# Reversing the column order of the moving operand and the PSUM output in all three-part products

## The reference, cut to what matters

```python
def first_block(x, ...):                 # HGRN2 mixer + conv mixer, then a conv SwiGLU FFN
    z = einsum('btd,dc->btc', rmsnorm(x), w_in)          # 1024 x 3584
    ...                                                   # chunkwise HGRN2, causal convolutions
    x = x + rmsnorm(concat(mix_a, mix_b) @ w_out)         # 1024 x 1024
    u = causal_dwconv(rmsnorm(x) @ ffn_w_up)              # 1024 x 5632
    return x + rmsnorm((silu(gate) * val) @ ffn_w_down)   # 2816 x 1024

def second_block(x, ...):                # two layers, each with a FFN before and after its mixer
    for l in range(2):
        h = h + 0.5 * swiglu(rmsnorm(h), wg, wu, wd)      # 1024 x 2816 twice, 2816 x 1024
        h = h + (pool_mixer(u) if l == 0 else mla_attention(u, ...))
        h = h + 0.5 * swiglu(rmsnorm(h), wg, wu, wd)
    return rmsnorm(h)
```

## Time and profile before

| | |
|---|---|
| median of 3 runs | 2345.33 us |
| the 3 runs | 2345.01, 2345.33, 2349.53 us |
| span of the profiled execution, first to last instruction | 2346.3 us |
| PE (matmul) busy | 2321.3 us, 99% |
| PEld (weight load) busy | 2020.8 us, 86% |
| VectorE busy | 1661.6 us, 71% |
| ScalarE, GpSimd busy | 1008.6 us (43%), 842.6 us (36%) |
| share of the DMA engines | about 29% of the span |
| granted TensorE clock | 0.997 of full speed |

### The profile page before, as it was taken

How to read it: one execution, slowest core, us unless ns; L and a number is a source line. 1 busy time by engine, 2 the same in 40 slices (tenths; PEclk the granted TensorE clock), 3 DMA queues, 4 the chain that set the end, 5 groups by cost and what they waited for, 6 DMA issues and landing times.

```text
span 2346.3 us, 33505 instructions
## 1 busy us (share of the span) xinstructions
PE 2321.3 (99%) x13510; PEld 2020.8 (86%) x13510; DVE 1661.6 (71%) x1666; ACT 1008.6 (43%) x1277; POOL 842.6 (36%) x441
## 2 busy tenths in 40 slices
PE   8999999999999999999999999999999999999998
PEld 7889788888789999989899879899967778799997
DVE  5687587772489687669696769696777743696874
ACT  5324443442355344554354454353543342453443
POOL 1320222121046456348256328355311001474551
PEclk9999999999999999999999999999999999999999
DMA  5221232323323332323332332333221122233322
GB/s 162 86 72 55 72 108 89 107 85 99 103 72 107 110 108 86 105 79 105 107 122 83 91 117 91 108 113 103 91 68 40 45 72 90 90 99 109 117 86 85
DMA packets 220050, 219.29 MB, mean 93 GB/s; under 512 B 10897, under 2 KB 217360, under 8 KB 219920
## 3 DMA queue, kind: packets, MB, share of 16 engines
q1 hardware_dynamic: 218992, 215.27, 28.9%
q10 hardware_dynamic: 928, 2.17, 0.4%
HBM read 213.22 MB, written 2.10 MB: 92 GB/s over the span
## 4 chain that ended last, share of the span: by engine, by line
PE 85%; POOL 6%; DVE 3%; DMA 2%; ACT 2%; issue 1%; SPq 0%; DVEq 0%; ACTq 0%; POOLq 0%
PE bank L1356 16%; PE bank L1358 15%; PE bank L1357 15%; PE bank L1350 10%; PE bank L1352 10%; PE bank L1351 10%; POOL sums L668 2%; POOL raw L669 2%; PE bank L1994 2%; PE bank L2041 2%; PE bank L1997 1%; POOL sums L671 1%; PE bank L1485 1%; POOL sums L673 1%; DMA raw<-in_ffn_pre_wu_dram 1%
## 5 line engine op out<-in xcount | busy, mean ns | idle before, releaser
L1350 PE MATMUL bank<-Xhi,wlo 128*128 128x256 f32 (+1 forms) x1283 | 374.1, 292 | 4.2 <-DVE Xlo L2342 2.8
L1351 PE MATMUL bank<-Xlo,whi 128*128 128x256 f32 (+1 forms) x1283 | 373.1, 291 | 0.0
L1352 PE MATMUL bank<-Xhi,whi 128*128 128x256 f32 (+1 forms) x1283 | 373.0, 291 | 0.0
L668 POOL TENSOR_TENSOR sums<-raw 128x512 f32<-128x512 f32 x72 | 147.4, 2047 | 429.2 <-DMA raw<-in_ffn_post_wg_dram 162.9
L1031 ACT ACTIVATE whi<-raw 128x2048 fp32r<-128x2048 f32 x72 | 138.3, 1920 | 371.5 <-PE bank L1358 223.9
L1350 PE MATMUL bank<-Xhi,sxlo 128*128 128x256 f32 (+1 forms) x960 | 280.8, 292 | 0.3
L1351 PE MATMUL bank<-Xlo,sxhi 128*128 128x256 f32 (+1 forms) x960 | 278.9, 291 | 0.0
L1352 PE MATMUL bank<-Xhi,sxhi 128*128 128x256 f32 (+1 forms) x960 | 278.9, 291 | 0.0
L1350 PEld LDWEIGHTS bank<-Xhi,wlo 128*128 128x128 f32 x1283 | 241.8, 188 | 11.7 <-issue 4.5
L1351 PEld LDWEIGHTS bank<-Xlo,whi 128*128 128x128 f32 x1283 | 241.7, 188 | 6.4 <-issue 0.5
L1352 PEld LDWEIGHTS bank<-Xhi,whi 128*128 128x128 f32 x1283 | 241.8, 188 | 5.8
(11 more groups left out here) (378 smaller groups left out, 5567.6 us busy)
## 6 DMA issues: line engine op xcount, KB each, us to landing
raw<-in_ffn_w_up_dram SPq DMA_DIRECT2D x22, 1024.0 KB, 5.1
raw<-in_ffn_pre_wg_dram SPq DMA_DIRECT2D x22, 1024.0 KB, 5.3
raw<-in_ffn_pre_wu_dram SPq DMA_DIRECT2D x22, 1024.0 KB, 5.4
raw<-in_ffn_post_wg_dram SPq DMA_DIRECT2D x22, 1024.0 KB, 5.3
raw<-in_ffn_post_wu_dram SPq DMA_DIRECT2D x22, 1024.0 KB, 5.3
raw<-in_ffn_pre_wd_dram SPq DMA_DIRECT2D x24, 768.0 KB, 4.8
raw<-in_ffn_post_wd_dram SPq DMA_DIRECT2D x24, 768.0 KB, 4.9
raw<-in_w_in_dram SPq DMA_DIRECT2D x13, 1024.0 KB, 5.0
```

Source lines behind the costliest of these rows:

```text
L668: nc.gpsimd.tensor_tensor(s1, a21, a22, ALU.add).then_inc(adds_done[h], 1)
L1350: nc.tensor.matmul(bank, wl, x, start=first, stop=False, skip_group_check=True)
L1351: nc.tensor.matmul(bank, w, xl, start=False, stop=False, skip_group_check=True)
L1352: return nc.tensor.matmul(bank, w, x, start=False, stop=last, skip_group_check=True)
```

## The change

In both helpers the output and the two moving operands are replaced by views with the columns in opposite order. Column 511 (or 255) is streamed first and written first, column 0 last. The stationary operands, the number and order of instructions, their waits and signals, and the tiles that they touch are the same; the result in each PSUM column is the same sum of the same terms.

```diff
+            def backwards(t):
+
+                return t[:, ::-1]
+
             def product(bank, w, wl, x, xl, first, last):
 
+                bank, x, xl = backwards(bank), backwards(x), backwards(xl)
                 nc.tensor.matmul(bank, wl, x, start=first, stop=False, skip_group_check=True)
                 nc.tensor.matmul(bank, w, xl, start=False, stop=False, skip_group_check=True)
                 return nc.tensor.matmul(bank, w, x, start=False, stop=last, skip_group_check=True)
 
             def three(bank, whi_, wlo_, xhi, xlo, first, last):
 
+                bank, xhi, xlo = backwards(bank), backwards(xhi), backwards(xlo)
                 nc.tensor.matmul(bank, wlo_, xhi, start=first, stop=False)
                 nc.tensor.matmul(bank, whi_, xlo, start=False, stop=False)
                 return nc.tensor.matmul(bank, whi_, xhi, start=False, stop=last)
```

## The result

The changed kernel takes 2381.18 us (median of 4 runs, 2380.21 to 2384.08) against 2346.99 us before (4 runs): the ratio is 1.0148, with a 95% interval of 1.0137 to 1.0160. The forecast was no change; rival B, a dearer stream but not by half, is what came. First the page of the changed kernel, its lines on busy time and clock, which answer to the earlier trace rows.

The account below looks back on a forecast made before the run. The prediction took PE's queue of matmuls as the bound. Nothing was added or removed and the handing over and falling stream were priced at 0, giving no change: 2345.5 us, range 2338 to 2480 us.

Parts of the forecast that it names:

- rival B: Reversed PE stream: falling order makes stalls twice as frequent, 140 us more (2486 us), anything from 5 up counting; chance 0.13.
- What bounds the kernel: Whole kernel: PE's matmul queue, busy 2321.3 of 2346.3 us, so its pace goes into the time one to one.
- The count: Both helpers: 12306 matmuls touched, 6372 streaming 256 columns and 5934 streaming 512.
- The pace: Touched matmuls: starts 226.4 ns apart at 512 columns and 116.5 ns at 256, together 2085.8 us.
- Handing over between matmuls and other kinds of matmul, cost 0: PE between successive matmuls, and where another kind follows a reversed one: bank order and waits stay as before, cost 0.
- So I take 0 for the stream: SBUF read and PSUM write of reversed matmuls: no price, carried over from VectorE; bounds 140 us less to 1805 more.
- The PSUM rule: PSUM write: 8-byte lines, non-contiguous output slows matmuls significantly; whether step -1 counts as contiguous was left open.
- The SBUF rule: SBUF read: 16-byte lines, second access to a line at full rate, so a falling fp32 read costs nothing.
- Rival A: Reversed PE stream: falling columns handled singly at 0.833 ns each, 1805 us more, about 4150 us; chance 0.16.
- rival C: Touched matmuls: stalls from rising moving reads meeting rising weight loads go away, down to 2206 us; chance 0.04.

Follow-up runs that it names:

- e3: Kernel before with the reversal, read and write, in helper `three` alone: 2375.90 us, ratio 1.0128.
- e5: Kernel before with the reversal, read and write, in helper `product` alone: 2350.22 us, ratio 1.0014.
- e2: Kernel before with only the PSUM columns written backwards, the moving operand read in rising order: 2347.26 us, ratio 1.0005.
- e9: Kernel before, rising, `Xhi` and `Xlo` meant for 28 words from the weights; rounded gaps put them at 32 and 40 from `whi` and `wlo`: 2362.89 us, ratio 1.0072.
- e8: Kernel before, rising, with `Xhi` and `Xlo` at 48 words modulo 64 from the weights instead of 8: 2350.93 us, ratio 1.0020.
- e12: Kernel before, rising, with `Xhi` and `Xlo` at 15 words modulo 64 from the weights instead of 8: 2341.50 us, ratio 0.9978.

## Why the prediction missed its likeliest case, point by point

- **What bounds the kernel: right.** PE's pace went into the time one to one: 33.7 us more busy, 33.4 us more span, no new wait.
- **The count: right**, 6372 and 5934 matmuls. **The pace: too coarse.** Two places were read and taken for all. The 759 matmuls of 512 columns on `Xhi` and `Xlo` already ran at 233.3 ns instead of 226.4, and that difference, visible in the trace of before, was the clue to the whole case.
- **Handing over between matmuls and other kinds of matmul, cost 0: right** as far as the runs can tell. The halves add up within their intervals (e3, e5), and the plain records keep their pace.
- **"So I take 0 for the stream": wrong; this is the step that failed.** It carried VectorE's insensitivity to a step of two over to PE. Measured over all starts in the two traces, the term is 30.7 us for the 512-column matmuls of `three` (5088 of them, on average 6.0 ns dearer, a little less than the 6.6 between settled paces, since some of before are disturbed too), 0.7 us for those of `product`, and 4.3 us for its 256-column ones (on average 117.5 and 118.2 ns): 35.7 us; the 192 matmuls of `three` with 256 columns got 0.3 us quicker. The span grew by 33.4 us; where the other 2 us were saved is not traced.
- **The two rules of the Trainium skill.** The PSUM rule did not apply (e2). The SBUF rule ("Advanced Engine Details and Errata", "Memory Cachelines"), that a second access to the same line is at full rate, is not contradicted, as the falling read lost 3% and not half; it says nothing of two reads beside each other, and their distance moved the pace by those 3%.
- **Rival A (pairing lost, 4150 us): excluded.** **Rival B: came, at a quarter of its full price**, but with a sentence beside it that was wrong: "I can name nothing in the order of addresses that would add a stall". I had named it under rival C, moving reads meeting weight loads, and dismissed it since the starts are evenly spaced. A settled cycle can be evenly spaced (226 and 227 ns at distance 0), so that is no evidence against the two reads affecting each other. Rival A's premise, that something takes two columns at a time, no run shows.
- **The range held, the chances did not put the weight where it belonged**: slower had 0.29. That 2381 us lies inside is owed to rival B's width of 5 to 140 us, not to a mechanism that I had seen.

What is shown: the price is on the read side, it is there with PE alone at work, of the three kinds of data tried only one-pass fp32 pays it, and at 512 columns it goes by the distance of the moving and the stationary operand modulo 64 words together with the direction; in the full kernel, losing the distance costs nearly what the reversal costs, and the two do not add. What stays open: how the two reads hinder each other, why the same distance can settle at two paces, and whether a falling read is quicker at the odd distances that were not tried. At 512 columns the surplus does not shrink with fewer stationary columns, so a mere count of colliding accesses does not explain it, and a stationary operand read the other way round was not tried.

## What to carry to other kernels

When PE is the bound and streams one-pass fp32, read the start-to-start time of neighbouring matmuls for every moving tile apart, not in one place; equal widths at different paces point to the placement of tiles. Then try the distance of moving and stationary tiles modulo 64 words, before and after any change of layout or access order: here it is worth 1.4% of the whole time, and padding alone can give or take it. Read the addresses of the tiles from the built program, since a gap may be rounded up and shift everything behind it (e9), and measure in the kernel itself, since the 256-column paces of matmuls alone did not carry over (e8). At 512 columns the falling order cost nothing at a distance where the rising one was slow already; it lost what a good distance had given.

## What the runs showed of the hardware that I had not expected

- 512 fp32r columns take 226.7, 228.9, 230.0, 231.1, 233.3, 236.7 or 240.0 ns in settled groups, and means in between, with the distance, the direction and the width of the stationary operand, and in a few places differently in two sweeps; 226.7, 230.0, 233.3, 236.7 and 240.0 are 3.3 ns apart, eight periods of 2.4 GHz. The least was 13.4 ns over one column per period.
- PE took ten matmuls to settle after a disturbance in one group (64 words, rising), so short groups do not show the pace.
- Writing PSUM in falling order is free (ratio 1.0005), and plain fp32 and bf16 read in falling order at their full pace.
- A tile that starts on an odd word from an aligned one (15 words, e12) did not slow the kernel through the engines that write it: it was the fastest version.
